# First chunk behind four norms on x times gain, scaled from the bank; unit sums split in high and low

## The reference

```python
for i in range(2):
    h = rmsnorm(x, norm_mix[i])
    x = x + (even_mixer(h, ...) if i == 0 else odd_mixer(h, ...))
    x = x + conv_ffn(rmsnorm(x, norm_ffn[i]), ...)

# even_mixer: z = h @ w_in, cut in aq ak av ag ar bq bk bv
#   log_a = log_sigmoid(ar @ w_a2 + b_a) / 16; oa = gated linear attention(aq, ak, av, log_a)
#   bq, bk = rmsnorm over each head of 64;  ob = differential attention(bq, bk, bv), normed per head
#   (concat(rmsnorm(oa) * silu(ag), ob)) @ w_out
# odd_mixer: z = h @ w_in; q, k = rmsnorm over each head of 128; three dilated windows; @ w_out
# conv_ffn: u = h @ w_up; causal convolution of 3 taps + bias; (silu(gate) * val) @ w_down
```

## Time and profile before

| | us |
|---|---|
| three runs | 1378.12, 1373.53, 1373.29 |
| median | 1373.53 |
| the profiled execution | 1372.37 |
| its span, first to last instruction | 1370.6 |
| mean granted clock of PE, share of full | 0.995 |

### The profile page before, as it was taken

How to read it: one execution, slowest core, us unless ns; L and a number is a source line. 1 busy time by engine, 2 the same in 40 slices (tenths; PEclk the granted TensorE clock), 3 DMA queues, 4 the chain that set the end, 5 groups by cost and what they waited for, 6 DMA issues and landing times.

```text
span 1370.6 us, 25612 instructions
## 1 busy us (share of the span) xinstructions
PE 1326.3 (97%) x10934; PEld 1286.2 (94%) x10934; DVE 980.6 (72%) x1218; ACT 735.6 (54%) x944; POOL 319.3 (23%) x165
## 2 busy tenths in 40 slices
PE   7999999999999999999999999999999999999997
PEld 6888999999999899999989989999999998999997
DVE  6965799975577489997658776999765876644443
ACT  6647666555565465654555655554355555655331
POOL 5000054600000015540024002763002400177200
PEclk9999999999999999999999999999999999999998
DMA  8333667775655457776344545899834444555550
GB/s 296 126 123 121 263 251 263 267 266 185 214 178 177 139 185 277 288 261 222 127 177 156 174 160 221 285 319 347 343 120 177 162 159 155 179 186 185 185 185 31
DMA packets 40865, 278.72 MB, mean 203 GB/s; under 512 B 4656, under 2 KB 5168, under 8 KB 9264
## 3 DMA queue, kind: packets, MB, share of 16 engines
q1 hardware_dynamic: 33696, 226.23, 46.5%
q10 hardware_dynamic: 7056, 50.86, 10.1%
HBM read 276.02 MB, written 1.05 MB: 202 GB/s over the span
## 4 chain that ended last, share of the span: by engine, by line
PE 88%; DVE 5%; ACT 4%; issue 1%; DMA 0%; SPq 0%; DVEq 0%; ACTq 0%
PE bank L837 24%; PE bank L839 24%; PE bank L838 24%; PE bank L803 2%; PE bank L796 2%; PE bank L797 2%; DVE low L1543 2%; ACT high L1147 1%; PE bank L815 1%; PE bank L817 1%; PE bank L816 1%; PE bank L880 1%; PE bank L1112 1%; PE bank L1083 1%; PE bank L992 1%
## 5 line engine op out<-in xcount | busy, mean ns | idle before, releaser
L1543 DVE TENSOR_TENSOR low<-raw,high 128x2048 fp32r<-128x2048 f32 (+3 forms) x223 | 497.5, 2233 | 221.1 <-ACT high L1147 217.7
L837 PE MATMUL bank<-op_high,low 128*128 128x256 f32 (+2 forms) x1928 | 545.9, 283 | 3.4 <-ACT mv L1221 2.5
L838 PE MATMUL bank<-op_low,high 128*128 128x256 f32 (+2 forms) x1928 | 537.9, 279 | 0.0
L839 PE MATMUL bank<-op_high,high 128*128 128x256 f32 (+2 forms) x1928 | 537.9, 279 | 0.0
L1147 ACT ACTIVATE high<-raw 128x2048 fp32r<-128x2048 f32 (+3 forms) x223 | 407.0, 1825 | 145.5 <-PE bank L839 132.9
L837 PEld LDWEIGHTS bank<-op_high,low 128*128 128x128 f32 (+2 forms) x1928 | 363.2, 188 | 9.0 <-issue 6.3
L838 PEld LDWEIGHTS bank<-op_low,high 128*128 128x128 f32 (+2 forms) x1928 | 360.4, 187 | 3.1 <-issue 2.4
L839 PEld LDWEIGHTS bank<-op_high,high 128*128 128x128 f32 (+2 forms) x1928 | 361.8, 188 | 0.2
L837 PE MATMUL bank<-act_high,low 128*128 128x256 f32 x864 | 241.8, 280 | 0.0
L839 PE MATMUL bank<-act_high,high 128*128 128x256 f32 x864 | 241.0, 279 | 0.0
L838 PE MATMUL bank<-act_low,high 128*128 128x256 f32 x864 | 240.8, 279 | 0.0
(11 more groups left out here) (303 smaller groups left out, 1781.5 us busy)
## 6 DMA issues: line engine op xcount, KB each, us to landing
raw<-stream SPq DMA_DIRECT2D x197, 1024.0 KB, 4.9
adaw<-ada ACTq DMA_DIRECT2D x28, 1024.0 KB, 6.3
adax<-ada ACTq DMA_DIRECT2D x20, 1024.0 KB, 5.1
raw<-stream SPq DMA_DIRECT2D x10, 768.0 KB, 5.7
raw<-stream SPq DMA_DIRECT2D x10, 512.0 KB, 3.5
raw<-stream SPq DMA_DIRECT2D x2, 640.0 KB, 4.2
x<-xT SPq DMA_DIRECT2D x2, 512.0 KB, 4.4
out<-h SPq DMA_DIRECT2D x1, 1024.0 KB, 3.9
```

What stands on the lines that cost most here:

```text
L837: pe.matmul(o, wl[:, w], oh[:, k, :], start=one, stop=False, skip_group_check=True)
L838: pe.matmul(o, wh[:, w], ol[:, k, :], start=False, stop=False, skip_group_check=True)
L839: mm = pe.matmul(o, wh[:, w], oh[:, k, :], start=False, stop=end, skip_group_check=True)
L1543: dve.tensor_tensor(low[m % SPLIT][:, at:w], raw[m % RAW][:, at:w], high[m % SPLIT][:, at:w], ALU.subtract).then_inc(S["low_ready"], 1)
```

## The change

Four parts:

1. The first chunk behind norms 0 to 3 (bq0, up0g0, od000, up1g0, in `FIRST`) no longer takes the normed operand. It takes x times gain, rounded by ACT into a buffer of its own (`GAIN_HIGH`) and with the rest from DVE (`GAIN_LOW`). The norm's last sums on PE stand in the middle of this chunk. When the products are done, DVE multiplies the bank by `rn` into h[:, 0:2] (`first_scaled`), and ACT and DVE go on from there. The second chunk (bk0, up0v0, od001, up1v0) is now the one that takes the normed pairs as they come. The filler matmuls before these four norms' chunks are gone.
2. The stages `xg` of pairs 0 to 3 of norms 1 to 3 have two more roundings on ACT and two more subtractions on DVE each, and DVE has them in its queue where the order has `xg`.
3. The start is reordered: the gains come by ACT's queue, rounding of x times gain comes first, 20 matmuls on it (WARM) run before the first products, and the products with the gain that the norm needs come later (`gains`). In the stream ar stands behind bk0 and not before it; its stages (`ar`, `la`, `la_exps`) move back by a chunk.
4. The squares of a unit are made twice by ACT (fp32 and rounded), DVE subtracts (`unit_split`), and PE sums high and low with two rounded matmuls instead of one fp32.

The core of the diff:

```diff
-BUSY = 10
+BUSY, WARM = 10, 20
...
-    for name, base, tm in (("bq0", o["bq"], 0), ("ar", o["ar"], 0), ("bk0", o["bk"], 0), ("bv0", o["bv"], 1), ("bq1", o["bq"] + 256, 0),
+    for name, base, tm in (("bq0", o["bq"], 0), ("bk0", o["bk"], 0), ("ar", o["ar"], 0), ("bv0", o["bv"], 1), ("bq1", o["bq"] + 256, 0),
...
         MLA_OUT = (OB, NB)
-        BEHIND_NORM = ("bq0", "up0g0", "od000", "up1g0", "cq0a", "fa0_0", "cq1a", "fa1_0")
+        FIRST = {"bq0": 0, "up0g0": 1, "od000": 2, "up1g0": 3}
+        GAIN_HIGH = (XH, AH[:, 13:21, :], GH2, AH[:, 13:21, :])
+        GAIN_LOW = (XL, AL[:, 13:21, :], GL2, AL[:, 13:21, :])
+        first_out = h[:, 0:2, :]
+        BEHIND_NORM = ("bk0", "up0v0", "od001", "up1v0", "cq0a", "fa0_0", "cq1a", "fa1_0")
...
                     st_("square", (i, pair)), st_("square_add", (i, pair))
-                    if i < 8 and pair < 3:
+                    if i < 8 and (pair < 3 or i < 4):
                         st_("xg", (i, pair))
                     pair += 1
                 if after is not None:
                     after()
-            st_("sumsq", (i, 3))
+            if i >= 4:
+                st_("sumsq", (i, 3))
             if i == 3:
                 st_("low", "odo1")
...
         st_("trig")
-        for p in range(4):
+        for p in range(2):
+            st_("xg", (0, p))
+        for p in range(2):
             st_("square", (0, p)), st_("square_add", (0, p))
-        for p in range(4):
+        for p in range(2, 4):
             st_("xg", (0, p))
-        st_("sumsq", (0, 2)), st_("sumsq", (0, 3))
-        st_("first_split"), st_("norm", 0)
-        c("bq0"), c("ar"), st_("ar")
-        c("bk0", split=False), st_("la"), st_("unit", 0), high_low("bk0")
-        c("bv0", split=False), st_("la_exps"), st_("unit", 1), st_("lam"), high_low("bv0")
-        c("bq1", split=False), st_("high", "bq1"), sw("diff", 0, 1), st_("low", "bq1")
+        st_("first_split")
+        for p in range(2, 4):
+            st_("square", (0, p)), st_("square_add", (0, p))
+        st_("second_split"), st_("gains"), st_("norm", 0), c("bq0")
+        c("bk0", split=False), st_("unit", 0), high_low("bk0")
+        c("ar"), st_("ar")
+        c("bv0", split=False), st_("la"), st_("unit", 1), st_("lam"), high_low("bv0")
+        c("bq1", split=False), st_("la_exps"), st_("high", "bq1"), sw("diff", 0, 1), st_("low", "bq1")
...
+            if name in FIRST:
+                return S["first_scaled"], FIRST[name] + 1
...
+                    pe.wait_ge(S["gain_high"], 1)
+                    for _ in range(WARM):
+                        pe.matmul(ps[bank_of(ch)][:, 0, :], oh[:, 0, 0:P], oh[:, 0, :], start=True, stop=True)
...
-                    if name in BEHIND_NORM:
+                    if name in BEHIND_NORM[4:]:
                         for _ in range(BUSY):
                             pe.matmul(out_of(0), wh[:, 0:P], wl[:, 0:TOK], start=True, stop=True)
                     for at in range(0, len(turns), 2):
                         some = turns[at:at + 2]
+                        if name in FIRST and at == len(turns) // 2:
+                            if n == 0:
+                                sumsq((0, 2))
+                            sumsq((FIRST[name], 3))
...
-                pe.wait_ge(S["unit_squares"], u + 1)
+                pe.wait_ge(S["unit_split"], u + 1)
                 claim(bank)
                 if u == 0:
-                    pe.wait_ge(S["consts_in"], 16)
-                pe.matmul(ps[bank][:].rearrange("p a b -> p (a b)"), col("ones64" if u < 4 else "ones"),
-                          sq[u % 2][:].rearrange("p a b -> p (a b)"), start=True, stop=True).then_inc(S["unit_sums"], 1)
+                    pe.wait_ge(S["ones_rounded"], 1)
+                o, ones = ps[bank][:].rearrange("p a b -> p (a b)"), ones_r[:, int(u >= 4), :]
+                pe.matmul(o, ones, sq_high(u).rearrange("p a b -> p (a b)"), start=True, stop=False)
+                pe.matmul(o, ones, sq_low(u).rearrange("p a b -> p (a b)"), start=False, stop=True)\
+                    .then_inc(S["unit_sums"], 1)
...
-            def squares_of(u, bank):
+            def squares_of(u, src):
                 if u >= 2:
                     act.wait_ge(S["unit_sums"], u - 1)
-                act.activation(sq[u % 2][:], ps[bank][:], ACT.Square).then_inc(S["unit_squares"], 1)
+                act.activation(sq[u % 2][:], src, ACT.Square)
+                act.activation(sq_high(u), src, ACT.Square).then_inc(S["unit_squares"], 1)
+                if u == 0:
+                    act.wait_ge(S["consts_in"], 16)
+                    act.activation(ones_r[:, 0, :], col("ones64"), ACT.Copy)
+                    act.activation(ones_r[:, 1, :], col("ones"), ACT.Copy).then_inc(S["ones_rounded"], 1)
...
+            def high_of_gain(i, k):
+                g, _ = gain_and_shift(i)
+                return act.activation(GAIN_HIGH[i][:, k, :], x[:, k, :], ACT.Copy, scale=g[:, k:k + 1])
+
             def xg(a):
                 i, p = a
                 if i == 0:
+                    if p == 0:
+                        act.dma_start(params[:, 0:32], params_d[:, 0:32]).then_inc(S["gains_in"], 16)
+                        act.wait_ge(S["gains_in"], 16)
+                    act.wait_ge(S[f"x_in{p // 2}"], 16)
+                if p == 3 and i:
                     return
-                if p == 2:
-                    act.wait_ge(S["squares_added"], i + 1)
-                times_gain(i, 2 * p)
-                times_gain(i, 2 * p + 1).then_inc(S["xg_ready"], 1)
+                if i < 4:
+                    high_of_gain(i, 2 * p)
+                    high_of_gain(i, 2 * p + 1).then_inc(S["gain_high"], 1)
+                if i:
+                    if p == 2:
+                        act.wait_ge(S["squares_added"], i + 1)
+                    times_gain(i, 2 * p)
+                    times_gain(i, 2 * p + 1).then_inc(S["xg_ready"], 1)
...
                     act.activation(h[:, 6, :], x[:, 6, :], ACT.Square).then_inc(S["square_half"], 1)
-                    if i < 8:
+                    if i < 4:
+                        high_of_gain(i, 6)
+                    elif i < 8:
                         times_gain(i, 6)
                     act.wait_ge(S["x_updated"], 4 * i)
                     act.activation(h[:, 7, :], x[:, 7, :], ACT.Square).then_inc(S["squares_ready"], 1)
+                    if i < 4:
+                        high_of_gain(i, 7).then_inc(S["gain_high"], 1)
+                        times_gain(i, 6)
                     if i < 8:
                         times_gain(i, 7).then_inc(S["xg_ready"], 1)
...
-                if i == 0:
-                    if p == 0:
-                        dve.wait_ge(S["gains_in"], 16)
-                    if p == 2:
-                        dve.wait_ge(S["squares_added"], 1)
-                    g, _ = gain_and_shift(0)
+                if i < 4:
+                    dve.wait_ge(S["gain_high"], 4 * i + p + 1)
+                    g, _ = gain_and_shift(i)
+                    for k in (2 * p, 2 * p + 1):
+                        ins = dve.scalar_tensor_tensor(out=GAIN_LOW[i][:, k, :], in0=x[:, k, :], scalar=g[:, k:k + 1],
+                                                       in1=GAIN_HIGH[i][:, k, :], op0=ALU.mult, op1=ALU.subtract)
+                    ins.then_inc(S["gain_low"], 1)
+
+            def gains(_):
+                dve.wait_ge(S["squares_added"], 1)
+                g, _ = gain_and_shift(0)
+                for p in range(4):
                     for k in (2 * p, 2 * p + 1):
                         ins = dve.tensor_scalar(XG[p][:, k % 2, :], x[:, k, :], g[:, k:k + 1], None, ALU.mult)
                     ins.then_inc(S["xg_ready"], 1)
+
+            def second_split(_):
+                low_upto(0)
+
+            def unit_split(u):
+                dve.wait_ge(S["unit_squares"], u + 1)
+                dve.tensor_tensor(sq_low(u), sq[u % 2][:], sq_high(u), ALU.subtract).then_inc(S["unit_split"], 1)
+
+            def gla_squares(hp):
+                unit_split(GLA_U[hp])
+
+            def diff_squares(i):
+                unit_split(DIFF_U[i])
...
+                src = first_out if name in FIRST else ps[b]
+                if name in FIRST:
+                    dve.wait_ge(S["products_done"], n + 1)
+                    dve.tensor_tensor(first_out, ps[b][:], rn[:].rearrange("p (a b) -> p a b", a=1)
+                                      .to_broadcast([P, 2, TOK]), ALU.mult).then_inc(S["first_scaled"], 1)
+                elif name.startswith("pa") and name.endswith("1"):
                     dve.wait_ge(S["merge_half"], int(name[2]) + 1)
                 elif ch["last"] and name.startswith(("aq", "ak", "evo", "odo", "down", "up", "uk", "pp", "pa", "wo", "fb")):
                     dve.wait_ge(S["products_done"], n + 1)
-                if name == "aq":
+                if name in units:
+                    unit_split(units[name])
```

(3 more changed lines are left out.)

66 lines of the change are left out of this document (41 added, 25 removed).

## The result

The changed kernel takes 1397.7 us (median of four runs, 1392.21 to 1406.33), the kernel before 1374.08 on the same chip (1373.29 to 1378.12). The ratio is **1.0209, 95% interval 1.0171 to 1.0246**: slower, some 28 us by the ratio, where I had said 17 and a range up to 1402. The two medians alone are 23.6 us apart (1.0172, the low end of that interval), and a second measurement further down gives 1.0167.

What follows compares the result with a forecast made beforehand. PE, busy 97% of the span, was taken as the bound, so only its waits or own work could pay. From 1372.4 us, 10.0 - 1.2 + 0.3 - 4.7 + 9.4 + 3.4 = +17.2 gave about 1390 us, range 1374 to 1402.

Steps and rivals of the forecast that it cites:

- the two large places: The start, 10.0 us lost by evo0, and norm 3, 9.4 us lost, where weight splits wait in DVE's queue.
- norm 2: Around od000 to od010: od000 starts earlier, but the gain waits at unit 8; od010 at 345.9, 0.3 us lost.
- the clock: PE restarts at 1.2 GHz after the two longest idles, before bk0 and up1g0: 3.4 us lost, 0 to 8 possible.
- norm 1: Around up0g0 to up0v1: PE waits 1.8 us for up0g1's split, yet 1.2 us are gained.
- start, up to evo0: First chunks through the first block's attention: bk0 starts at 26.4, scores reach DVE 9.5 us late; 10.0 us lost.
- units 9 to 19: Eleven covered unit sums as two rounded matmuls save 0.43 us each: 4.7 us gained.
- norm 3: Around up1g0 and up1v0: their splits come late in DVE's queue, up1v0 at 499.1 against 489.56; 9.4 us lost.
- rival B: At the start: the loss is absorbed, the later gates' chain still ending before the scores need it; 1378 us, chance 0.15.
- Rival D: Clock stays low in more places, at od010 and four stretches in the attention part: 1398 us, chance 0.15.
- Rival C: Splits of up1g0 and up1v0 done in time, PE runs on through the norms: 1352 us, chance 0.12.

Runs made afterwards that it cites:

- e4_ahead: Changed kernel with the next chunks' weight rounding and splitting put ahead of the norm pass at all four norms, same instructions: 1381.49 us, ratio 1.0084 to the kernel before.
- e2_no_norm3: Changed kernel with norm 3 done as before, up1g0 taking the normed operand, with fillers: ratio 1.0109 to the kernel before.
- e3_no_norm0: Changed kernel with the start as before: bq0 on the normed operand, ar ahead of bk0, gates' stages in old places. Ratio 1.0133 to the kernel before.
- e6_best: e4_ahead with start and norm 3 as before, od000 in a free bank, only units 8 to 19 in two parts: ratio 0.9975 to the kernel before, repeated 0.9992.
- e13_no_unit_split: Changed kernel with the unit sums as one fp32 matmul again, no second square and no subtract: ratio 1.0202 to the kernel before.
- e14_no_units_ahead: e4_ahead with the unit sums as one fp32 matmul again, no second square and no subtract: ratio 1.0084 to the kernel before.
- e1_units: Kernel before with only the two-part sums of the 20 units added: 1368.98 us against 1368.64, ratio 1.0004.
- e7_fill: Changed kernel with filler matmuls, results thrown away, in PE's four long waits (bk0, unit 8, up1g0, up1v0): 1388.42 us, ratio 1.0116 to the kernel before.

## Why the prediction was right and where it was wrong

The direction, the two large places and the mechanism were right: the weight splits stand behind the norm pass in DVE's queue. e4_ahead shows it (with ACT's roundings, which it moves too), e2_no_norm3 and e3_no_norm0 show the two places. Two steps failed, both below: norm 2, put at +0.3 us and measured at +3.8, and the clock, put at 3.4 us and worth about 8. No errors cancel: every row of the table came out above what I had, norm 1 by no more than 0.2 us. By offsets in the profiled executions, which sum to 27.0:

| step | predicted | measured |
|---|---|---|
| start, up to evo0, with one low-clock stretch | +10.0 + 1.7 | +12.8 |
| norm 1 | -1.2 | -1.0 |
| norm 2 | +0.3 | +3.8 |
| units 9 to 19 | -4.7 | -1.9 |
| norm 3, with one low-clock stretch | +9.4 + 1.7 | +12.1 |
| behind it | 0 | +1.2 |

- *The start.* bk0 was put at 26.4 and came at 29.0. The first half of bq0 still ran at 1.2 GHz up to 15.7 us, so the scale came at 19.2 instead of 17.7; the norm pass took 6.6 us, not 5.0, beside GpSimd. The scores came at 59.84 instead of 55.9. That such a delay goes through to evo0 undiminished was right, and rival B is refuted by the table above. That the 1 to 1.5 us of GpSimd would matter was in no version of mine, and they don't.
- *Norm 1.* Right to 0.2 us, and by the steps given: the split of up0g1 behind the norm pass, PE waiting 1.64 us for it (1.8 forecast).
- *Norm 2* is the step that failed: "od010 starts at 345.9". I let od000 start as soon as its operand was there. Its bank, though, is held by the last projection until x is updated. The profile names DVE's split as what ended that wait, but this ended at 341.5; what ended at 342.2, 0.1 us ahead of od000, is the update of x behind it in DVE's queue:

```profile
...
339.24 2.29 DVE L1607 TENSOR_TENSOR low<-raw,high 128x2048 fp32r<-128x2048 f32 x1 [3.61 <-ACT high L1184]
341.44 0.75 DVE L1692 TENSOR_TENSOR x<-bank,x 128x256 f32<-128x256 f32 x2
```

  e4_ahead keeps this wait of 1.17 us, e6_best, with another bank, has none. With the offset of 11.75 us taken off, od000 came 1.3 us later than forecast (330.5 for 329.2), the norm pass ended 1.4 later and od010 began 1.8 later (347.7 for 345.9): the scale, the split of od010 and unit 8's squares followed in the order I gave, only later. The 4.03 us of idle let the clock fall, and od011 has another 1.7 us of loss. Of the 4.7 us between od001 and od010, e13_no_unit_split keeps 3.6, so some 1.1 are the two-part sum; e4_ahead keeps 1.4, e14_no_units_ahead 0.2. The order is the larger part of the wait at unit 8, the squares add to it.
- *Units 9 to 19.* The two-part sum is 0.39 us shorter a chunk where PE is the bound. But ACT's second squares made a cover fail that I had called safe, the turned weights of the dilated attention:

```profile
...
413.08 0.52 PE L1041 MATMUL bank<-consts,DS 128*128 128x128 f32 x3 [0.78 <-ACT DT L1469]
...
429.35 0.52 PE L1041 MATMUL bank<-consts,DS 128*128 128x128 f32 x3 [0.81 <-ACT DT L1469]
```

  Neither wait is in the trace of before or of e13_no_unit_split, and both are in that of e1_units, whose one edit is the sums. I put them at 1.9 us with the restart of PE behind them; 0.9 us of the expected gain I can't place.
- *Norm 3.* By its own steps right to a microsecond: up1g0 5.3 us late was forecast and 4.0 measured, up1v0 9.5 and 10.4. The second low-clock stretch, at up1v0, is the rest.
- *The clock* is the term that was mis-sized. I counted two stretches, 3.4 us; the trace has one at each of the four idles, which together cost 8.3 us by e7_fill, and short ones near 835 and 1180 us that give the last line of the table (the second execution has neither). Rival D had this at 0.15. With it the sum is some 1395, still 4 us short of the profiled 1399.3, and these are about what norm 2 (1.8 without the clock) and the DT waits (1.9) add. Where the earlier trace rows showed a stretch behind 1.2 us of waiting, an idle of 4.5 us should have been charged as surely as one of 7.

The Trainium skill, TensorE: Matmul & The Clock Gate (What's actually happening), says that throttled is the default and that activity releases it. By that rule all four restarts run cold, and e7_fill, where matmuls of no use remove all four, agrees.

Rival C needed up1g0's split by 478 and up1v0's by 484. e4_ahead had both at 485.8, and even there norm 3 loses 4.1 us.

## What to carry to other kernels

Before a chunk is pulled ahead of a norm, read the queues of the engines that round and split its weights: filling PE's idle pays only if the next chunks' splits already stand ahead of the norm pass, and what PE gains it otherwise waits for right behind. Here each of the four new idles of 4 us and more was followed by a low clock, so charge such an idle with it. And where an engine is busy throughout a stretch, one time, that of the first work handed to it, forecast the end of the stretch to 1.3 us in eight traces of ten; the other two had more low clock behind it.
